# Two transformer layers and a delta-rule block on one core: modulation chunks moved to the feed-forward part, heads turned amid the v2 product, rotary halves swapped by transfers

## The chip, the cores and the metric

One core of a Trainium2 chip runs the whole program in one launch. Its engines are TensorE (PE in the profile), VectorE (DVE), ScalarE (ACT), GpSimd (POOL) and SyncE (SP, which issues most DMA transfers). The metric is the device time in microseconds, the median of several executions.

## What is computed

Two layers act on 256 tokens of width 1024, all in float32. Each has a mixer (a pooling branch and twelve attention heads of 64 in three dilation patterns), a feed-forward part of width 4096 and a gated embedding. A second block with a gated delta rule follows. It needs "modulation" columns, a product of two condition vectors with a weight of 1024 x 6144 that depends on nothing in the layers.

```python
def apply_partial_rotary(x, cos, sin):      # half = 8 of 64 columns
    x1 = x[..., :half]
    x2 = x[..., half:ROT_DIM]
    rot = jnp.concatenate([x1 * cos - x2 * sin, x2 * cos + x1 * sin], axis=-1)
    return jnp.concatenate([rot, x[..., ROT_DIM:]], axis=-1)
...
    for i in range(DEPTH):
        z = rmsnorm(h, norm1[i]) @ w_in[i]          # pool input, q, k, v
        q, k = rotary(q), rotary(k)
        attn_out = dilated_mixer(q, k, v)           # softmax within and across patterns
        h = h + jnp.concatenate([pool_out, attn_out], axis=-1) @ w_out[i]
        h = h + jnp.square(jax.nn.relu(rmsnorm(h, norm2[i]) @ w_up[i])) @ w_down[i]
        h = h + sigmoid(rmsnorm(h, norm3[i]) @ w_gate[i]) * (p[i] @ w_ple[i])
```

## The kernel before

**Weights as a stream.** Every weight is cut into chunks of 1 MB (`Stream`), loaded in one fixed order by SyncE's loop into four raw buffers (`RAW`). A load waits until the chunk four places earlier has been used up (`slot_free`). Most chunks are split: ScalarE writes a high part (`split_hi`, L521), DVE the low part (`split_lo`, L530), in two pieces of a half chunk each, into rings of four pieces (`PIECES`). PE then does three products per tile (high by high, low by high, high by low: L539 to L541), so a chunk is 48 matmuls of 256 columns, or 24 of 512. "Direct" chunks, those of the modulation weight and of the context, are multiplied from the raw buffer in full float32.

**Layer order.** Chunks 0 to 5 give q and k for three head pairs (`qk0` to `qk5`), 6 and 7 the first two thirds of v, 8 the pooling input u, 9 the last third of v (v2), 10 to 13 the output product, then up and down chunks of the feed-forward part alternate (14 to 45, `KIND`), then 46 to 51.

**Rotary.** ScalarE copies a product out of its bank (`z_raw`, L1737). PE multiplies it with a 128x128 matrix of 0, 1 and -1 (`rotate`, L1377), which swaps the two halves of eight rows and sets the sign. DVE multiplies the result with the sine table (`rotated`, L2156), GpSimd `z_raw` with the cosine table (L2546), DVE adds both (L2160). `z_raw`, `z_cos` and `z_sin` have two buffers each. PE does the rotation of product s behind product s + 1.

**Attention.** PE computes scores (L1386, L1387) into a ring of four banks (0 to 3, `low` and `CL`). DVE adds the mask and takes the maxima (`maxima`, L2168 to L2175), ScalarE the exponentials (`exps`, L1769), DVE scales them by weights for six heads at a time (`weights`, L2211). A table, `ATT_EXTRA`, and `attention_order` set what follows: "T" turns a head's probabilities on PE (L1295) and ScalarE copies them (L1792), "V" multiplies a head pair with v (L1438, L1440), ScalarE and DVE write the two parts of the result (L1800, L2265). Modulation work stands in the same order: "mod" is one chunk (L1317, two chunks are one pair), "modr" ScalarE's copy of a pair's rows (L1634), "modc" turns them into columns on PE (L1302), and DVE adds the bias (L2092). A second ring, banks 4 to 7 (`high` and `C`), serves the products, modulation and u. Layer 1's table has four context chunks in place of the modulation. `FFN_EXTRA` says what modulation work follows which chunk in layer 0's feed-forward part.

## Time and profile before

| what | us |
|---|---|
| median of three executions | 1394.09 (1393.87 to 1400.3) |
| profiled execution | 1391.02 |
| its span | 1389.0 |
| PE busy in it | 1302.8 |
| mean granted TensorE clock | 0.969 |

The span is the time from the first to the last instruction. Rows of the trace name an engine, a line of the kernel, the output and inputs by the program's names, and partitions x elements. A start is in microseconds from the span's start. Matmuls are pipelined and their ends are modelled, so steps are measured from start to start. "Idle before" in brackets is what the engine waited for.

### The profile page before, as it was taken

How to read it: one execution, taken by the hardware profiler on the slowest of the kernel's cores; microseconds unless marked ns; L12 is line 12 of the kernel's file. 1: busy time of each engine (PE TensorE's matmuls, PEld its weight loads, DVE VectorE, ACT ScalarE, POOL GpSimd, SP SyncE). 2: the span in 40 equal slices, each digit the busy share in tenths (PEclk: the TensorE clock that was granted, in tenths of full speed). 3: DMA queues.
4: the chain of work that ended last, by engine and by line, in shares of the span. 5: the costliest groups of instructions: out<-in, count | busy, mean ns of one | idle time of the engine just before them, and what ended most of it. 6: DMA issues, size and time to landing. Idle time of an engine off the chain costs nothing.

```text
span 1389.0 us, 22276 instructions
## 1 busy us (share of the span) xinstructions
PE 1302.8 (94%) x9222; PEld 1189.4 (86%) x9222; DVE 819.8 (59%) x1189; ACT 641.0 (46%) x950; POOL 124.6 (9%) x108
## 2 busy tenths in 40 slices
PE   7987999999999999789999989988889999999997
PEld 6964988888898889679999988988789998899996
DVE  6672464544685756676655586576644566654444
ACT  6353353443556635434444356454136453544443
POOL 0130000000002112140001030023310000000000
PEclk9997999999999999999999999999999999999999
DMA  9558467776554344234443444542004555355540
GB/s 320 164 189 267 141 221 242 242 245 227 178 181 152 92 138 136 91 122 152 152 152 123 159 145 122 152 122 92 30 1 135 183 173 179 130 189 190 190 151 31
DMA packets 163802, 218.74 MB, mean 157 GB/s; under 512 B 5016, under 2 KB 134902, under 8 KB 163574
## 3 DMA queue, kind: packets, MB, share of 16 engines
q1 hardware_dynamic: 161842, 215.15, 47.5%
q10 hardware_dynamic: 1860, 2.16, 0.5%
q8 instruction: 73, 1.20, 0.4%
q14 instruction: 27, 0.22, 0.1%
HBM read 216.26 MB, written 1.05 MB: 156 GB/s over the span
## 4 chain that ended last, share of the span: by engine, by line
PE 64%; issue 20%; DVE 6%; ACT 2%; POOL 2%; DMA 2%; DVEq 2%; POOLq 2%; ACTq 0%; SPq 0%
PE bank L539 17%; PE bank L540 17%; PE bank L541 17%; PE bank L602 2%; DVE w_lo L530 1%; PE bank L1317 1%; DMA w_raw<-in_w_mod 1%; PE bank L1295 1%; PE bank L1524 1%; PE bank L824 1%; PE bank L1377 1%; PE bank L812 1%; PE bank L1302 1%; DVEq L2171 1%; DMA arena<-in_vec_rows 1%
## 5 line engine op out<-in xcount | busy, mean ns | idle before, releaser
L530 DVE TENSOR_TENSOR w_lo<-w_raw,w_hi 128x1024 fp32r<-128x1024 f32 (+1 forms) x350 | 423.4, 1250 | 167.8 <-ACT w_hi L521 161.5
L539 PE MATMUL bank<-act_hi,w_hi 128*128 128x256 f32 x1744 | 505.0, 290 | 18.2 <-DVE act_lo L2139 5.1
L540 PE MATMUL bank<-act_lo,w_hi 128*128 128x256 f32 x1744 | 498.5, 286 | 0.0
L541 PE MATMUL bank<-act_hi,w_lo 128*128 128x256 f32 x1744 | 498.1, 286 | 0.0
L521 ACT ACTIVATE w_hi<-w_raw 128x1024 fp32r<-128x1024 f32 (+1 forms) x350 | 348.9, 1041 | 102.8 <-PE bank L541 89.9
L539 PEld LDWEIGHTS bank<-act_hi,w_hi 128*128 128x128 f32 x1744 | 339.7, 195 | 33.7 <-issue 19.4
L540 PEld LDWEIGHTS bank<-act_lo,w_hi 128*128 128x128 f32 x1744 | 339.9, 195 | 1.0 <-issue 0.5
L541 PEld LDWEIGHTS bank<-act_hi,w_lo 128*128 128x128 f32 x1744 | 339.5, 195 | 0.0
L539 PE MATMUL bank<-w_hi,side_hi 128*128 128x512 f32 (+1 forms) x392 | 151.1, 386 | 0.0
L540 PE MATMUL bank<-w_lo,side_hi 128*128 128x512 f32 (+1 forms) x392 | 148.6, 379 | 0.0
L541 PE MATMUL bank<-w_hi,side_lo 128*128 128x512 f32 (+1 forms) x392 | 148.4, 379 | 0.0
L1839 ACT ACTIVATE arena<-bank 128x512 f32<-128x512 f32 x32 | 19.1, 596 | 164.6 <-PE bank L541 164.6
L539 PEld LDWEIGHTS bank<-w_hi,side_hi 128*128 128x128 f32 x392 | 74.7, 191 | 14.6 <-issue 2.1
L541 PEld LDWEIGHTS bank<-w_hi,side_lo 128*128 128x128 f32 x392 | 74.4, 190 | 13.7
L540 PEld LDWEIGHTS bank<-w_lo,side_hi 128*128 128x128 f32 x392 | 74.7, 191 | 12.7 <-issue 0.5
L2296 DVE TENSOR_TENSOR arena<-arena 128x512 f32<-128x512 f32 x32 | 22.2, 695 | 105.3 <-ACTq L1840 105.3
L539 PE MATMUL bank<-side_hi,w_hi 128*128 128x256 f32 x208 | 63.7, 306 | 4.8 <-issue 2.7
L540 PE MATMUL bank<-side_lo,w_hi 128*128 128x256 f32 x208 | 60.2, 289 | 0.0
L541 PE MATMUL bank<-side_hi,w_lo 128*128 128x256 f32 x208 | 60.1, 289 | 0.0
L2546 POOL TENSOR_TENSOR arena<-arena 128x512 f32<-128x512 f32 x12 | 15.5, 1295 | 388.7 <-DVEq L2227 349.5
L539 PEld LDWEIGHTS bank<-side_hi,w_hi 128*128 128x128 f32 x208 | 41.3, 198 | 7.6 <-issue 5.2
L540 PEld LDWEIGHTS bank<-side_lo,w_hi 128*128 128x128 f32 x208 | 41.3, 199 | 1.7 <-issue 1.7
(323 smaller groups left out, 1540.8 us busy)
## 6 DMA issues: line engine op xcount, KB each, us to landing
w_raw<-in_w_in SPq DMA_DIRECT2D x40, 1024.0 KB, 5.8
w_raw<-in_w_up SPq DMA_DIRECT2D x32, 1024.0 KB, 6.4
w_raw<-in_w_down SPq DMA_DIRECT2D x32, 1024.0 KB, 5.0
w_raw<-in_w_mod SPq DMA_DIRECT2D x24, 1024.0 KB, 5.3
w_raw<-in_w_ffn_in SPq DMA_DIRECT2D x22, 1024.0 KB, 5.2
w_raw<-in_w_gate SPq DMA_DIRECT2D x20, 1024.0 KB, 5.3
w_raw<-in_w_ffn_out SPq DMA_DIRECT2D x11, 1024.0 KB, 5.3
w_raw<-in_w_out SPq DMA_DIRECT2D x8, 1024.0 KB, 8.0
```

The source lines that it names most:

```text
L521: nc.scalar.activation(whi[:, slot, 0:n], raw[:, st.slot(name), n * half:n * (half + 1)], ACT.Copy).then_inc(hi_ready, 1)
L530: nc.vector.tensor_tensor(wlo[:, slot, 0:n], raw[:, st.slot(name), n * half:n * (half + 1)], whi[:, slot, 0:n].bitcast(F32), ALU.subtract) ...
L539: nc.tensor.matmul(o, ahi, bhi, start=start, stop=False, skip_group_check=True)
L540: nc.tensor.matmul(o, ahi, blo, start=False, stop=False, skip_group_check=True)
L541: return nc.tensor.matmul(o, alo, bhi, start=False, stop=stop, skip_group_check=True)
L602: mm = nc.tensor.matmul(ps[bank][:, T * m:T * (m + 1)], raw[:, st.slot(name), at:at + P], act[:, k, :], start=k == 0, stop=k == KT - 1)
L812: mm = nc.tensor.matmul(ps[b][:, P * hh:P * (hh + 1)], h4(g_A[:, n, :])[:, hh, :], d_.x_new_of(n, hh, lv), start=True, stop=True)
L824: mm = nc.tensor.matmul(ps[b][:, P * hh:P * (hh + 1)], h4(z_sm[:, n, :])[:, hh, :], d_.t_new_of(n, hh, lv), start=True, stop=True)
L1295: tr = lambda o, x: nc.tensor.transpose(o, x, ident)
L1839: free(nc.scalar.activation(relu[j % 2], pair(b), ACT.Relu), b)
L2296: v.tensor_tensor(relu2[j % 2], relu[j % 2], relu[j % 2], ALU.mult).then_inc(S("relu2"), 1)
L2546: g.tensor_tensor(z_cos[s % 2], z_raw[s % 2], wide(tab_c, 2), ALU.mult).then_inc(S("z_cos"), 1)
```

## The change

The pairs 2 to 5 of the modulation (eight chunks, four row copies, four column turns) leave layer 0's attention and stand in its feed-forward part, where twelve chunks were before; there two chunks now go with every three weight chunks, from chunk 15 on, in place of two with every four from chunk 16. Pairs 0 and 1 stay. The v2 product is cut in two halves with the first two head turns in between, and these two write banks of the high ring. The last four heads' maxima come ahead of the copy of u on DVE, and their exponentials on ScalarE behind the first two head copies. The split of output chunks 10 and 11 in layer 0 is later. The first output product waits for its inputs one by one. The rotation on PE is gone: SyncE issues four transfers of 8 partitions x 512 elements per product from `z_raw` to `z_sin`, the sign is in the sine table, and `z_sin` is cleared once at the start.

```diff
+ROPE_MOVES = 16 * 4
...
-        ("ident", P), ("ones", P), ("rot", P), ("eps", 1), ("ln_q", 1), ("eps2", 1), ("even", 1), ("inv_freq", 1), ("pad", 1), ("mod_sum", 2),
+        ("ident", P), ("ones", P), ("eps", 1), ("ln_q", 1), ("eps2", 1), ("even", 1), ("inv_freq", 1), ("pad", 1), ("mod_sum", 2),
...
-            inv[m, 0] = np.float32(THETA) ** np.float32(-2.0 * (d % half) / ROT)
...
+            inv[m, 0] = (-1.0 if d < half else 1.0) * np.float32(THETA) ** np.float32(-2.0 * (d % half) / ROT)
...
-    out = [("v2", 0)] + extra.get("v2", [])
+    out = [("v2", 0)]
     for i, (b, g) in enumerate(pairs):
         out += [("T", HPG * g + 2 * b), ("T", HPG * g + 2 * b + 1)]
-        if i:
+        if i == 0:
+            out.append(("v2", 1))
+        else:
             out.append(("V", 2 * pairs[i - 1][1] + pairs[i - 1][0]))
-        if i == 4:
+        if i == 5:
...
-    {"v2": mod(0, 1, 2, 3), 0: [("modr", 0)] + mod(4, 5), 1: [("modr", 1), ("modc", 0)] + mod(6, 7),
-     2: [("modr", 2), ("modc", 1)] + mod(8, 9), 3: [("modr", 3), ("modc", 2)] + mod(10, 11),
-     4: [("modr", 4), ("modc", 3)], 5: [("modr", 5), ("modc", 4)], "V": [("modc", 5)]},
...
+    {1: mod(0, 1), 2: [("modr", 0)] + mod(2, 3), 3: [("modc", 0)], 4: [("modr", 1)], 5: [("modc", 1)]},
+    {1: [("ctx", 0)], 2: [("ctx", 1)], 3: [("conv", 0), ("ctx", 2)], 4: [("conv", 1), ("ctx", 3)], 5: [("conv", 2)],
+     "V": [("conv", 3), ("ba", 0)]})
...
-for j in range(6, MOD_PAIRS):
-    for at, entry in ((0, ("mod", 2 * j)), (2, ("mod", 2 * j + 1)), (3, ("modr", j)), (4, ("modc", j))):
-        FFN_EXTRA[0].setdefault(16 + 4 * (j - 6) + at, []).append(entry)
+for j in range(2, MOD_PAIRS):
+    for at, entry in ((0, ("mod", 2 * j)), (1, ("mod", 2 * j + 1)), (1, ("modr", j)), (2, ("modc", j))):
+        FFN_EXTRA[0].setdefault(15 + 3 * (j - 2) + at, []).append(entry)
...
-            early = 8 if layer == 0 else 3
+            early = 4 if layer == 0 else 3
...
-        def project_tokens(pe, name, bank):
-
-            for half in range(2):
+        def project_tokens(pe, name, bank, halves=(0, 1)):
+            for half in halves:
...
-                def rotate(s):
-                    wait("z_raw", s + 1, 6)
-                    b = CL(f"rot{s}")
-                    full(nc.tensor.matmul(ps[b][:, :], col("rot", 0, P),
-                                          z_raw[s % 2].rearrange("p m t -> p (m t)"), start=True, stop=True), b)
...
-                    else:
-                        if s == 1:
-                            ssq("ssq1", 1, CL("ssq1"))
-                        rotate(s - 1)
+                    elif s == 1:
+                        ssq("ssq1", 1, CL("ssq1"))
...
-                rotate(5)
...
-                        b = CL(f"pT{x}")
+                        b = C(f"pT{x}") if i < 2 else CL(f"pT{x}")
...
-                        b = C("v2")
-                        project_tokens(pe, (layer, 9), b)
+                        if x == 0:
+                            C("v2")
+                        project_tokens(pe, (layer, 9), banks.bank((layer, "v2")), (x,))
...
+                def cat_ready(f):
+                    first = max(f, 1)
+                    wait("cat_act", 1 + max(CAT_ORDER.index(x) for x in [0] + list(range(2, first + 1))), 7)
...
-                        if j == 0:
-                            wait("cat_act", 7, 7)
-                        project(pe, (layer, s), lambda m: (b, T * m), KT, all_hi, all_lo)
+                        project(pe, (layer, s), lambda m: (b, T * m), KT, all_hi, all_lo,
+                                cat_ready if j == 0 else None)
...
-                        W(f"rot{s - 2}")
+                        act.wait_ge(S(f"z_turned{s % 2}"), ROPE_MOVES * (layer * 3 + s // 2))
...
-                exps(8, 12)
...
-                        if layer != CTX_LAYER and i == 5:
-                            split_hi(act, chunk(layer, 10))
-                        if i == (3 if layer == CTX_LAYER else 9):
+                        if layer != CTX_LAYER and i == 9:
+                            split_hi(act, chunk(layer, 10), (0,))
+                        if layer == CTX_LAYER and i == 5:
                             split_hi(act, chunk(layer, 11))
...
-                    elif kind == "v2":
+                    elif kind == "v2" and x == 1:
+                        exps(8, 12)
...
+                if layer != CTX_LAYER:
+                    split_hi(act, chunk(layer, 10), (1,))
+                    split_hi(act, chunk(layer, 11))
...
-                    b = W(f"rot{s}")
-                    free(v.tensor_tensor(z_sin[s % 2], pair(b), wide(tab_s, 2), ALU.mult), b)
+                    dve.wait_ge(S(f"z_turned{s % 2}"), ROPE_MOVES * (layer * 3 + s // 2 + 1))
+                    v.tensor_tensor(z_sin[s % 2], z_sin[s % 2], wide(tab_s, 2), ALU.mult)
...
                 weights(0)
-
+                maxima(8, 12)
                 done(8)
                 b = bank("u")
                 free(v.tensor_tensor(win[0][:, :, PADW:], pair(b), wide(rstd_w[:, 0:T], 2), ALU.mult), b)
                 dve.drain().then_inc(S("u_ready"), 1)
-                maxima(8, 12)
+                weights(1)
                 if layer == CTX_LAYER:
                     split_lo(dve, chunk(layer, 10))
-                weights(1)
                 n = 0
                 for kind, x in ATT[layer]:
                     if kind == "modc":
...
-                    if n == 3:
-                        split_lo(dve, chunk(layer, 11 if layer == CTX_LAYER else 10))
-                    if n == 6 and layer != CTX_LAYER:
+                    if n == 3 and layer == CTX_LAYER:
                         split_lo(dve, chunk(layer, 11))
+                    if n == 5 and layer != CTX_LAYER:
+                        split_lo(dve, chunk(layer, 10), (0,))
...
+                if layer != CTX_LAYER:
+                    split_lo(dve, chunk(layer, 10), (1,))
+                    split_lo(dve, chunk(layer, 11))
...
+            for x in z_sin:
+                g.memset(x, 0.0)
...
+            def turn_halves(layer, s):
+                sp.wait_ge(S("z_raw"), layer * 6 + s + 1)
+                if layer or s >= 2:
+                    sp.wait_ge(S("qk_ready"), layer * 6 + s - 1)
+                half = ROT // 2
+                for i in range(2):
+                    for to, of in ((0, half), (half, 0)):
+                        to, of = HEAD * i + to, HEAD * i + of
+                        sp.dma_start(z_sin[s % 2][to:to + half], z_raw[s % 2][of:of + half]).then_inc(
+                            S(f"z_turned{s % 2}"), 16)
+            turns = {st.at[layer, 0] + s + 6: (layer, s) for layer in range(DEPTH) for s in range(6)}
             for n, (name, _, _) in enumerate(st.chunks):
+                if n in turns:
+                    turn_halves(*turns[n])
```

On PE in layer 0's attention, around the first V product (L1438, L1440; banks of the ring are shown). Before:

```order
L1317 MATMUL bank4<-w_raw,silu_c_cols 32x512 x8
L1317 MATMUL bank5<-w_raw,silu_c_cols 32x512 x8
L1295 MATMUL bank0<-consts_sb,arena 128x128 x3
L1295 MATMUL bank1<-consts_sb,arena 128x128 x3
L1317 MATMUL bank6<-w_raw,silu_c_cols 32x512 x8
L1295 MATMUL bank2<-consts_sb,arena 128x128 x3
L1295 MATMUL bank3<-consts_sb,arena 128x128 x3
L1438 MATMUL bank0<-arena 64x256
L1440 MATMUL bank0<-arena 64x128
```

Of the changed kernel, from the first V product's end to the fourth head pair (L1291 is the turn, L1313 the modulation, L1425 and L1427 the V product):

```order
L1427 MATMUL bank0<-arena 64x128
L1313 MATMUL bank6<-w_raw,silu_c_cols 32x512 x8
L1291 MATMUL bank1<-consts_sb,arena 128x128 x3
L1291 MATMUL bank2<-consts_sb,arena 128x128 x3
L1425 MATMUL bank3<-arena 64x256
...
L1313 MATMUL bank7<-w_raw,silu_c_cols 32x512 x8
L1291 MATMUL bank0<-consts_sb,arena 128x128 x3
```

Six modulation chunks stood ahead of the third head before, none does now; the fourth pair's first turn takes the bank that the first V product filled.

On SyncE's queue, the loads of layer 0's q, k and v stage. Before:

```order
L2594 DMA w_raw<-in_w_in 128x8x256 x3
L2602 DMA consts_sb<-in_consts 128x4608
L2594 DMA w_raw<-in_w_in 128x8x256 x5
L2594 DMA w_raw<-in_w_mod 128x4x512 x8
L2594 DMA w_raw<-in_w_out 128x8x256
```

Of the changed kernel (L2592 is the load, L2606 the swap):

```order
L2615 DMA consts_sb<-in_consts 128x4608
L2592 DMA w_raw<-in_w_in 128x8x256
L2606 DMA arena<-arena 8x512 x4
...
L2592 DMA w_raw<-in_w_mod 128x4x512
L2606 DMA arena<-arena 8x512 x4
L2592 DMA w_raw<-in_w_mod 128x4x512 x3
L2592 DMA w_raw<-in_w_out 128x8x256 x4
```

Four swaps stand ahead of each load from the seventh chunk on, six times in all; the first is behind the tables and one load.

On the same queue, the loads of layer 0's feed-forward part. Before:

```order
L2594 DMA w_raw<-in_w_mod 128x4x512
L2594 DMA w_raw<-in_w_down 128x2x1024
L2594 DMA w_raw<-in_w_up 128x8x256
L2594 DMA w_raw<-in_w_mod 128x4x512
L2594 DMA w_raw<-in_w_down 128x2x1024
L2594 DMA w_raw<-in_w_up 128x8x256
```

Of the changed kernel:

```order
L2592 DMA w_raw<-in_w_mod 128x4x512
L2592 DMA w_raw<-in_w_up 128x8x256
L2592 DMA w_raw<-in_w_mod 128x4x512
L2592 DMA w_raw<-in_w_down 128x2x1024
L2592 DMA w_raw<-in_w_up 128x8x256
```

One load in three was a modulation chunk, two in five are now, and they come over ten rounds of three weight chunks.

## Rows read from the trace of the kernel before

**Rows 1.** The page: busy time and share of PE; the clock in 40 slices, tenths.

```profile
PE 1302.8 (94%) x9222; PEld 1189.4 (86%) x9222; DVE 819.8 (59%) x1189; ACT 641.0 (46%) x950; POOL 124.6 (9%) x108
...
PEclk9997999999999999999999999999999999999999
```

**Rows 2.** Stages: stretch, its us, busy us of each engine, clock, DMA share, GB/s.

```profile
83.80:137.70 53.90, 40.39 (x281) 24.01 (x281) 24.89 (x84) 21.24 (x53) 10.47 (x12) 0.79 0.75 254
137.70:164.70 27.00, 25.51 (x192) 25.32 (x192) 10.61 (x13) 7.80 (x10) 0.00 (x0) 0.90 0.48 150
176.40:300.00 123.60, 121.93 (x790) 102.11 (x788) 63.51 (x64) 55.13 (x67) 0.00 (x0) 1.00 0.70 238
474.70:523.60 48.90, 48.70 (x297) 42.35 (x296) 30.42 (x90) 21.90 (x54) 11.96 (x12) 0.97 0.38 119
```

**Rows 3.** Waits in 83.8 to 137.7: total us, times, longest.

```profile
PE bank L1317 <- DMA w_raw<-in_w_mod: 11.6, 4, 7.1
```

**Rows 4.** Timeline of PE, layer 0's attention: start, us, line, operation.

```profile
114.28 0.88 PE L1295 MATMUL bank<-consts_sb,arena 128*128 128x128 f32 x6
115.09 0.66 PE L1438 MATMUL bank<-arena 128*64 128x256 f32 x4
...
115.90 1.05 PE L1302 MATMUL bank<-consts_sb,arena 128*128 128x2 f32 x8
116.88 1.06 PE L1317 MATMUL bank<-w_raw,silu_c_cols 128*32 128x512 f32 x8
125.00 1.93 PE L1317 MATMUL bank<-w_raw,silu_c_cols 128*32 128x512 f32 x8 [7.05 <-DMA w_raw<-in_w_mod]
...
129.54 1.13 PE L1450 MATMUL bank<-arena,pool_blocks 128*128 128x256 f32 x4
...
137.71 0.55 PE L539 MATMUL bank<-act_hi,w_hi 128*128 128x256 f32 x1 [1.91 <-issue]
```

**Rows 5.** Timeline of DVE: scaling of six heads, last maximum, scaling again.

```profile
84.81 2.85 DVE L2211 TENSOR_SCALAR arena<-arena 128x128 f32<-128x128 f32 x12
...
92.95 0.36 DVE L2175 TENSOR_SCALAR arena<-arena 128x2 f32<-128x2 f32 x1
...
97.59 4.12 DVE L2211 TENSOR_SCALAR arena<-arena 128x128 f32<-128x128 f32 x12
```

**Rows 6.** Timeline of PE around one rotation in layer 0.

```profile
36.54 0.28 PE L541 MATMUL bank<-act_hi,w_lo 128*128 128x256 f32 x1
36.66 1.02 PE L1377 MATMUL bank<-arena,consts_sb 128*128 128x512 f32 x2
...
37.63 0.28 PE L540 MATMUL bank<-side_lo,w_hi 128*128 128x256 f32 x1
```

**Rows 7.** Timeline of PE, last scores of layer 0.

```profile
81.78 0.46 PE L1386 MATMUL bank<-arena 64*128 64x128 f32 x2 [1.16 <-DVE arena L2169]
```

**Rows 8.** Timeline of DVE, low split of the fourth chunk.

```profile
35.38 2.35 DVE L530 TENSOR_TENSOR w_lo<-w_raw,w_hi 128x1024 fp32r<-128x1024 f32 x2
```

**Rows 9.** DMA issues to 240 us with landing; all raw loads of 14 to 60.

```profile
consts_sb<-in_consts SPq DMA_DIRECT2D x1, 2304.0 KB, 13.4
...
consts_sb<-in_consts SPq DMA_DIRECT2D x1, 196.0 KB, 2.5
...
DMA to landing us min/median/max: 5.1/6.4/14.4
```

**Rows 10.** Timeline of PE, feed-forward part of layer 0.

```profile
285.74 0.95 PE L1302 MATMUL bank<-consts_sb,arena 128*128 128x2 f32 x8
286.62 1.06 PE L1317 MATMUL bank<-w_raw,silu_c_cols 128*32 128x512 f32 x8
287.62 0.39 PE L539 MATMUL bank<-act_hi,w_hi 128*128 128x256 f32 x1
```

**Rows 11.** Timeline of PE, layer 1 behind the sixth product.

```profile
447.01 1.10 PE L1377 MATMUL bank<-arena,consts_sb 128*128 128x512 f32 x2 [1.99 <-ACT arena L1748]
```

**Rows 12.** Waits in layer 1's attention, 474.7 to 523.6.

```profile
ACT w_hi L521 <- DMA w_raw<-in_w_out: 4.1, 1, 4.1
```

More of the change, by code:

```diff
@@ L93, in const_tables @@
     put("ones", 1.0)
-    rot = np.zeros((P, P))
     half = ROT // 2
@@ L98, in const_tables @@
         d = m % HEAD
-        if d < half:
-            rot[m + half, m] = -1.0
-        elif d < ROT:
-            rot[m - half, m] = 1.0
         if d < ROT:
-            inv[m, 0] = np.float32(THETA) ** np.float32(-2.0 * (d % half) / ROT)
-    put("rot", rot)
+            inv[m, 0] = (-1.0 if d < half else 1.0) * np.float32(THETA) ** np.float32(-2.0 * (d % half) / ROT)
     put("inv_freq", inv)
@@ L282 @@
 V_ORDER = [x for k, x in ATT[0] if k == "V"]
+CAT_ORDER = [2 + x if k == "V" else 0 for k, x in ATT[0] if k in ("V", "pool")]
 def up_at(j):
```

2 lines of the change are left out of this document (removed).

## The prediction

> **What bounds the kernel now.** I read the page first: TensorE (PE) is busy 94% of a span of 1389.0 us, at full clock in all slices but one of the first four [rows 1]. So two things can move the time: work taken off PE, or gaps of PE that are closed. The table of stages says where the gaps are [rows 2]. Layer 0's attention (v2 product to the first output product, 83.8 to 137.7) lasts 53.9 us, of which PE is busy 40.4 at a mean clock of 0.79; the same stage of layer 1 lasts 48.9 us, PE busy 48.7. The feed-forward part of layer 0 is gapless (121.9 of 123.6 us), with the DMA engines at 0.70. So layer 0's attention is the hole. Its waits name the cause: PE waited 11.6 us for modulation chunks to land, 7.1 us of it at 125.0 [rows 3, 4]. The other 2 us of stillness are before 137.71 [rows 4]. The rest of the loss is the clock: row 125.00 shows two passes of a chunk at 1.93 us, row 116.88 the same work at 1.06 (1.2 against 2.4 GHz) [rows 4]. Twelve megabytes of modulation weights pass through four raw buffers there, beside a softmax that needs few loads.
>
> **1. Eight of twelve modulation chunks and four of six column turns leave layer 0's attention.** What is left there is bound by something else, so I walk the new order on the old time axis. Layer 0's stage starts when maxima free the banks of the last scores, at 83.76, as now. VectorE (DVE) scales the first six heads at 84.81 to 87.66, then takes the last four maxima at once (the u copy, 0.7 us, is moved behind them), which costs the same as now and keeps them near 93; the scaling of the last six heads starts at 97.59 now and ends 4.12 later, at 101.7 [rows 5]. PE meanwhile does both halves of v2, three head pairs, two V products and four modulation chunks. Its fourth pair needs heads that are scaled, and the bank of the first V product (four claims back on a ring of four banks), which DVE frees only behind all of that scaling: so it starts near 101.7, maybe 1 us earlier. From there PE has three head pairs at 0.81 (114.28 to 115.09), four V products at 0.81 (115.09 to 115.90), two column turns at 0.98 (115.90 to 116.88) and the pool product at 1.13 [rows 4]: 2.4 + 3.2 + 2.0 + 1.1 = 8.7 us. The last hand-off (ScalarE's high part, DVE's low part, with half of the first output chunk's split, about 1.2 us, queued ahead of it on DVE) adds 2. Together 101.7 + 8.7 + 2.0 = 112.4, or a stage of 28.6 us in place of 53.9: **-25.3**. Ends: if the scaling isn't what binds, PE's own work remains, v2 5.8 (48 slots of 0.12, the step from 36.54 to 36.66 [rows 6]) plus six pairs, six V, four chunks at 1.0, two turns and the pool, 22.6 us: -31. If the clock falls in the gaps, the tail of 8.7 takes about 1.8 times as long (1.93 against 1.06) and the waits with it: 36 us, -18.
>
> The output products after it ran 27.0 us with a granted clock of 0.90 [rows 2], since PE came from a standstill. With less of that I take **-1.0** (0 to -2.5).
>
> **2. They arrive in the feed-forward part.** PE is gapless there, so each is paid in full: a chunk 1.0 us (286.62 to 287.62), a column turn 0.88 (285.74 to 286.62) [rows 10]. 8 x 1.0 + 4 x 0.88 = **+11.5**. Is there room to load them? Five loads of 1.05 MB now go with three PE steps: 3 x 5.67 (a pair of up and down takes 11.3) + 2 x 1.0 + 0.9 = 19.9 us, so 263 GB/s. The stage moves 238 GB/s at a share of 0.70 [rows 2], 340 at a full share; so the share rises to 0.77. With four raw buffers a load is issued as soon as the fourth chunk before it is split or used, which I work out as 9 us or more before its own split, against 5.1 to 6.4 us that most loads take to land [rows 9]. I take no stall; if each of the ten periods loses 1 us, +10. ScalarE's copy of the rows now waits for the second chunk at once, ahead of the split of the next-but-one weight chunk: about 1.6 us of a slack of 3.
>
> **3. The rotary swap leaves PE.** A rotation costs PE 36.66 to 37.63, less one slot of 0.12 for the product's matmul between: 0.85 us [rows 6]; there are six per layer. ScalarE's z_raw copy stays; after it four transfers of 8 partitions x 2 KB swap rows, then DVE multiplies as before. In layer 0 five of the six lie ahead of the first v chunk's end: 5 x 0.85 = 4.25 us. The sixth gives nothing: from that end a chain over ScalarE and DVE (values, split, maxima) sets when the last scores find a bank, PE waits 1.16 us for it at 81.78 already [rows 7], and it would only wait longer. Against that stands the start. SyncE's queue issues the first swap near 25.5 behind the tables, which take 13.4 us to land, and behind a weight chunk (14.4 at most) issued at 20.6 [rows 9]; so I expect it at 33 to 35.5. DVE stands at it, and behind it in DVE's queue is the low split of the fourth weight chunk, which starts at 35.38 even now [rows 8] and takes 1.2 for its first half. PE, 0.85 us earlier, wants it at 35.8. So its first half is ready at 36.6 at best and 38.2 at worst (35.5 and two vector steps of 0.7 to 0.9 behind the swap, then 1.2): a new gap of 0.8 to 2.4 us, I take 1.6. Net **-2.65** (-3.5 to -1.8).
>
> No row shows a transfer from SBUF to SBUF. The smallest load with a landing, 196 KB, took 2.5 us, the slowest of 1 MB 14.4 [rows 9]. I take 3 to 5 us, nearer to the small one, since in the steady state the load ahead of it on the queue was issued 3 us before. DVE can wait until 7.5 us after the issue before the split behind it is late, so this is hidden. The Trainium skill, DMA: Bandwidth & Descriptors, "Anatomy of one DMA", gives about 2 us of fixed cost for a DMA on GpSimd's path, mostly the write receipt; by it the sum would be the same. The same page, "Queues, rings and completion order", says that each engine takes a ring's descriptors in order, which speaks against the change: the swap can't overtake the tables. No row here shows small transfers behind large ones; by that rule alone the gap would be the 2.4 us end, and the total 0.8 us longer.
>
> In layer 1 four rotations lie ahead of the sixth product: 3.4, of which 0.5 goes because the fourth chunk's split is just in time there too. The fifth waited 1.99 us for ScalarE at 447.01 [rows 11], and that and its 0.85 vanish from PE; but the attention's start is again set by the chain over values, splits and maxima, of which only about 0.4 shrinks. So the stage starts 3.3 us earlier, **-3.3** (-6 to -1), not 7.1. What is late next is the bank of the last scores, as in layer 0.
>
> **4. Layer 1's attention in its new order.** The same PE work is done (48.7 of 48.9 busy). The context chunks start later, so output chunk 11 lands later; ScalarE waits 4.1 us for it even now [rows 12], hidden under a context product of 7 us. I count **0** (-1 to +2), and if that cover is short by a load, up to +2.
>
> **The sum.** -25.3 - 1.0 + 11.5 - 2.65 - 3.3 + 0 = -20.75. The profiled execution took 1391.0, which gives 1370.3. It lies 3.1 us under the median of the three runs, 1394.1, and I keep that distance: **1373.3 us**.
>
> **Rivals.**
> - *The loads collide in the feed-forward part.* For it: 263 GB/s wanted against 238. Against: share 0.77. It costs 1 us in each of ten periods: 1383.
> - *Attention is a softmax chain with a cold clock.* For it: 0.79 in this stage [rows 2], and the new order has PE waits near 92 and 100. The stage takes 36 us, 7.5 more, and the output stage gains nothing: 1382.
> - *The tail is shorter still.* If scaling runs without GpSimd beside it (2.85 against 4.12 for the same twelve instructions [rows 5]) and hand-offs hide: 5 us less, 1368.
> - *Slower: swaps land late.* DVE's queue holds the split of the chunk three ahead behind each swap. If a swap lands L us after its issue, that split is late once L passes 7.5; the delay feeds the next z_raw three products later. At L = 14.4, the slowest load here, each round of three products loses 6.9 us. Twelve swaps are four rounds: +27.6, and the sum gives 1401. For it: one queue with the 1 MB loads. Against: those take 5.1 to 6.4 us, and only the first meets the tables.
> - *The chunks' removal does nothing because they fill waits that remain.* Then 1373.3 + 25.3 - 8 = 1391. Against: 11.6 us of waits on exactly these loads [rows 3].
>
> **Chances.** Forecast with its own bounds 0.75, collision 0.07, cold chain 0.07, shorter tail 0.04 (1363 to 1369), fills 0.03, slower swaps 0.04. The range must leave out no more than 2 in 10 and takes in both ends of the attention stage: 1364 to 1384. Half a per cent, about what a measurement tells from no change, is 7 us: faster than 1387 in 0.93, within in 0.03, slower in 0.04.
>
> **What would show it.** The stage of layer 0's attention at 28 to 29 us with no wait on w_mod, and the fourth head pair waiting for DVE. In the feed-forward part, periods of three steps near 19.9 us and the granted clock at 1.00. No 128x512 rotation on PE; a PE wait for w_lo of 1 to 2 us near 36; DVE's rotary product waiting for the first swap only. PE's wait in the last scores longer than 1.16 in both layers. I am wrong if PE waits for w_mod in the feed-forward part, if SyncE's swaps land later than 7.5 us, or if layer 0's attention stays above 36 us.

## The result, and the profile after

| kernel | median us (range) | before, same chip | ratio (95%) |
|---|---|---|---|
| changed, first measurement | 1379.85 (1378.0 to 1383.3) | 1395.9 | 0.9893 (0.987 to 0.9916) |
| changed, again (e1) | 1381.9 (1379.6 to 1387.0) | 1397.4 | 0.9908 (0.9882 to 0.9934) |

The change makes the kernel 1.0% faster: 13 to 15 us by the ratios, 15 to 16 by the medians. The forecast was 1373.3, in a range of 1364 to 1384. So the direction and the range held, but the time lies 6.5 us above the forecast, and of the 20.75 us of the sum 5 to 8 did not come. The executions of the kernel before spread from 1387.7 to 1400.6 over the chips used (one of 3209.6 us, in the slow state, is left out), and their mean granted clock goes with it (0.969 to 0.974 up to 1392.7, 0.962 to 0.967 from 1397.2 on). The profiled one, 1391.0, lies at the low end, and the profiled one of the changed kernel, 1383.3, at the high end of its own. So the two traces differ by 7.7 us where the medians differ by 16. Sizes of single stages below come from traces; what a whole kernel is worth comes from the ratios.

The stages of the changed kernel, columns as in [rows 2]. They are, in turn: first product to the first v product of layer 0, on to its v2 product, layer 0's attention, its output products, a piece of its feed-forward part, layer 1's attention, and the first output product of layer 1.

```profile
15.99:57.86 41.87, 39.21 (x299) 38.92 (x300) 29.89 (x31) 22.83 (x30) 7.65 (x5) 0.96 0.77 253
57.86:84.15 26.29, 24.86 (x195) 22.25 (x193) 19.15 (x59) 15.51 (x42) 1.85 (x1) 1.00 0.51 163
84.15:116.90 32.75, 24.88 (x186) 18.48 (x185) 22.51 (x75) 17.07 (x48) 10.88 (x12) 0.90 0.40 129
116.90:141.65 24.75, 23.25 (x192) 23.08 (x193) 14.41 (x17) 9.58 (x12) 0.00 (x0) 1.00 0.65 207
155.00:280.00 125.00, 124.43 (x812) 102.57 (x811) 61.82 (x66) 53.67 (x66) 0.00 (x0) 1.00 0.79 266
460.53:513.07 52.54, 49.12 (x297) 42.27 (x297) 33.56 (x92) 22.28 (x56) 12.51 (x12) 0.98 0.39 121
513.07:521.05 7.98, 7.98 (x50) 7.98 (x51) 3.28 (x12) 4.79 (x6) 2.48 (x3) 0.72 0.00 1
```

Layer 0's attention went from 53.9 us to 32.75, at a granted clock of 0.90 in place of 0.79. Layer 1's, which was gapless at 48.9, went to 52.54. All waits of PE of 0.6 us or more in layer 0's attention of the changed kernel (total us, times, longest):

```profile
PE bank L1291 <- DVE act_lo L2258: 5.0, 1, 5.0
...
PE bank L535 <- DVEq L2266: 1.5, 1, 1.5
...
PE bank L1313 <- DVE arena L2234: 0.7, 1, 0.7
...
PE bank L1438 <- DVE act_lo L2258: 0.6, 1, 0.6
```

The 11.6 us for w_mod [rows 3] are gone. In their place stands one wait of 5.0 us: the transpose of the fourth head pair needs the bank of the first V product, which DVE frees only behind its scaling of the last six heads. That scaling, on DVE's timeline, with the same work of the first six heads ahead of it; the third row is one of three small steps between:

```profile
85.20 2.84 DVE L2205 TENSOR_SCALAR arena<-arena 128x128 f32<-128x128 f32 x12
...
93.72 0.69 DVE L2234 TENSOR_TENSOR arena<-bank,rstd 128x512 f32<-128x512 f32 x1
...
95.82 1.03 DVE L2192 TENSOR_TENSOR arena<-arena 128x4 f32<-128x4 f32 x1
...
98.26 6.15 DVE L2205 TENSOR_SCALAR arena<-arena 128x128 f32<-128x128 f32 x12
104.33 0.97 DVE L2258 TENSOR_TENSOR act_lo<-bank,act_hi 128x256 fp32r<-128x256 f32 x2
```

Twelve equal instructions take 2.84 us once and 6.15 the other time; before, the second set took 4.12 [rows 5]. The u copy (93.72) releases GpSimd's window sums, which ran from 94.61 to 106.5 and so beside all of it. Before, they ran from 88.45 to 100.0: the first five us beside the maxima, only the last 2.4 beside the scaling. GpSimd's timeline before, then after:

```profile
88.45 4.83 POOL L2552 TENSOR_TENSOR arena<-arena 128x512 f32<-128x512 f32 x4 [29.76 <-DVEq L2241]
...
96.62 3.36 POOL L2562 TENSOR_TENSOR arena<-arena 64x256 f32<-64x256 f32 x4
```

```profile
94.61 4.82 POOL L2550 TENSOR_TENSOR arena<-arena 128x512 f32<-128x512 f32 x4 [33.99 <-DVEq L2235]
...
103.28 3.27 POOL L2560 TENSOR_TENSOR arena<-arena 64x256 f32<-64x256 f32 x4
```

PE behind its wait, and the first three us there in the columns of [rows 2]: the granted clock was 0.50.

```profile
104.89 1.51 PE L1291 MATMUL bank<-consts_sb,arena 128*128 128x128 f32 x6 [5.03 <-DVE act_lo L2258]
106.33 1.13 PE L1425 MATMUL bank<-arena 128*64 128x256 f32 x4
```

```profile
104.89:107.82 2.93, 2.93 (x14) 1.90 (x15) 0.42 (x1) 0.98 (x2) 1.55 (x3) 0.50 1.09 348
```

Layer 0's start did not get shorter: 68.12 us from the first product to v2 before, 68.16 after. DVE stood at the first swap, and PE behind it (DVE's timeline, then PE's, then SyncE's queue with the four transfers of the first swap and of the second):

```profile
36.28 0.69 DVE L2150 TENSOR_TENSOR arena<-arena 128x512 f32<-128x512 f32 x1 [3.75 <-DMA arena<-arena]
...
37.67 3.45 DVE L526 TENSOR_TENSOR w_lo<-w_raw,w_hi 128x1024 fp32r<-128x1024 f32 x2
```

```profile
39.03 0.35 PE L535 MATMUL bank<-side_hi,w_hi 128*128 128x256 f32 x1 [2.54 <-DVE w_lo L526]
```

```profile
25.50 4.99 SPq L2606 DMA_DIRECT2D arena<-arena  x4
31.52 0.38 SPq L2592 DMA_DIRECT2D w_raw<-in_w_in  x1
31.95 2.65 SPq L2606 DMA_DIRECT2D arena<-arena  x4
```

And layer 1's attention got two waits of PE and one long wait of ScalarE for w_out, which was 4.1 [rows 12]:

```profile
ACT w_hi L517 <- DMA w_raw<-in_w_out: 13.9, 1, 13.9
...
PE bank L598 <- issue: 2.2, 1, 2.2
...
PE bank L1291 <- DVE act_lo L2258: 1.2, 1, 1.2
```

### The profile page after: what moved, and what is told of

Same layout as the page of the kernel before. It is cut to its first block, busy times and chain, and to the rows that moved or that the text cites. A ratio compares the mean times of both kernels' runs of the same rounds, so it can differ in the third digit from the quotient of the medians.

```text
span 1381.5 us, 22278 instructions
## 1 busy us (share of the span) xinstructions
PE 1296.9 (94%) x9198; PEld 1188.4 (86%) x9198; DVE 826.3 (60%) x1189; ACT 640.7 (46%) x950; POOL 127.8 (9%) x110
## 4 chain that ended last, share of the span: by engine, by line
PE 60%; issue 21%; DVE 8%; ACT 3%; DVEq 2%; POOL 2%; POOLq 2%; DMA 2%; ACTq 1%; SPq 0%
PE bank L535 17%; PE bank L537 16%; PE bank L536 16%; DVE w_lo L526 2%; PE bank L598 2%; PE bank L1313 1%; PE bank L820 1%; PE bank L1291 1%; PE bank L1515 1%; DVEq L2165 1%; PE bank L808 1%; ACT w_hi L517 1%; DMA arena<-in_vec_rows 1%; DVE arena L2205 1%; PE bank L1298 1%
## 5 line engine op out<-in xcount | busy, mean ns | idle before, releaser
L535 PEld LDWEIGHTS bank<-act_hi,w_hi 128*128 128x128 f32 x1744 | 339.6, 195 | 31.0 <-issue 19.9
L2544 POOL TENSOR_TENSOR arena<-arena 128x512 f32<-128x512 f32 x12 | 18.6, 1560 | 367.5 <-DVEq L2221 331.6
```

Of the source, the lines that this page charges most:

```text
L535: nc.tensor.matmul(o, ahi, bhi, start=start, stop=False, skip_group_check=True)
L2544: g.tensor_tensor(z_cos[s % 2], z_raw[s % 2], wide(tab_c, 2), ALU.mult).then_inc(S("z_cos"), 1)
```

## The experiments

My theory after the result: the moved chunks are the gain; the swaps gave little because PE only arrives earlier at what ScalarE and DVE set; and the shortfall is two things that the new order did, DVE's queue in layer 0 and everything in layer 1. The rivals stand in the expectations. All runs are compared by their ratio to the kernel before on the same chip. The interval of each ratio is about 0.0025 to either side, 3.5 us, so a difference between two kernels is known to some 5 us only. Where it is smaller, the reading rests on the stages of the traces.

**e1, the changed kernel again.** No edit.

> The changed kernel once more, unchanged, beside the kernel before. The two profiles differ by 7.5 us, the medians by 16. Theory 'the profiled executions lie at opposite ends of the scatter': the median comes out at 1378 to 1382 again, 14 to 17 us under before, and the stages of a second profile repeat within 0.5 us except for waits on DMA (layer 1's attention 52.5, its first output product 8.0). Rival 'the profile is right and the first four times were lucky': the medians differ by 8 to 10 us.

1381.9 us, 15.4 under before by the medians, 12.9 by the ratio: the first theory. Layer 1's attention repeats (52.7). Layer 0's took 34.2, which is 1.4 longer, and first product to v2 67.35, 0.8 shorter, so stages repeat to about 1.5 us and not to the 0.5 that I expected.

**e3, chunks only.** In the kernel before, the new tables of modulation steps and nothing else:

```diff
-    {"v2": mod(0, 1, 2, 3), 0: [("modr", 0)] + mod(4, 5), ...
+    {1: mod(0, 1), 2: [("modr", 0)] + mod(2, 3), 3: [("modc", 0)], 4: [("modr", 1)], 5: [("modc", 1)]},
...
-for j in range(6, MOD_PAIRS):
+for j in range(2, MOD_PAIRS):
```

> The kernel before with only the modulation chunks and column turns of layer 0 moved to its feed-forward part (positions as in the changed kernel); the v2 product stays whole and first, all maxima and exponentials ahead of it as before, rotation on TensorE. Theory 'the chunks are the gain': layer 0's attention falls from 53.9 to 31 to 34 us, the output products win 2.3, the feed-forward part pays 12.6: the whole is 10 to 13 us faster than before, 1382 to 1385. Rival 'the cut of v2 and the heads amid it matter as much': attention stays at 38 to 40 us and the whole is 5 us faster than before, near 1390.

1388.1 us, ratio 0.9940: 8.4 us under before by the ratio, 9.3 by the medians, so more than half of the gain is the chunks alone, a little short of the 10 to 13 expected. Attention took 35.85 us in the trace, between the theory's 31 to 34 and the rival's 38 to 40. With the old order of heads DVE's second scaling took 4.12 us again, since the u copy ran ahead of the last maxima and GpSimd had started at 87.4.

**e2, the rotation back on TensorE.** The changed kernel without the swaps:

```diff
+                def rotate(s):
+                    wait("z_raw", s + 1, 6)
+                    b = CL(f"rot{s}")
+                    full(nc.tensor.matmul(ps[b][:, :], col("rot", 0, P), ...
...
-                if n in turns:
-                    turn_halves(*turns[n])
```

> The changed kernel with the rotary swap back as a product on TensorE (the transfers on SyncE's queue and DVE's wait for them are gone); the moved chunks and the order of attention stay. Theory 'in layer 0 the swaps gave nothing': PE pays 0.85 us for each rotation again but no longer waits 2.5 us for w_lo near 39 nor runs half a product at half clock (1.5 us), so the v2 product of layer 0 starts at 83.5 to 84.5 as in the changed kernel (84.15), layer 1 gives back 3.75 us, and the whole is 3 to 4 us slower than the changed kernel: near 1384. Rival 'as the prediction has it': the swaps are worth 2.65 + 3.3, so 6 us slower, 1386. Rival 'the small transfers also disturb the loads and the queue': same as the changed kernel or faster, 1378 to 1380.

1382.3 us, ratio 0.9907 against 0.9908: the medians show no loss, where 3 to 4 us were expected, and the interval leaves room for that. In the traces layer 0 takes 67.9 us from first product to v2 with the rotation and 67.35 without. Layer 1 shows where the gain goes. From layer 0's first output product to layer 1's first scores takes 328.85 us with the rotation, 321.16 without: 7.7 won. From there to v2 it is 20.43 against 22.70: 2.3 given back, 0.5 of it in a wait of PE for a split and most of the rest in the u product, whose first half ran at a clock near half (4.5 us in place of 3.0). This profiled execution lay 3 us over its own median, so I take the direction from it and not the size.

**e11, the swaps alone**, in the kernel before:

> The kernel before with only the rotary swap done by transfers; modulation chunks and the order of attention as before. Theory 'the swaps are worth little': taking them out of the changed kernel cost 0.4 us by the medians and 3.7 by the traces, all of it in layer 1; so 0.5 to 4 us faster than before, the first scores of layer 0 not earlier than 62.5 (64.0 before), layer 1's scores earlier by 6 to 7 us but its v2 product only by 4 to 5. Rival 'as the prediction has it': 6 us faster, 2.65 of it in layer 0. Rival 'the swaps cost elsewhere': same or slower.

1390.9 us, ratio 0.9969 (0.995 to 0.9988): 4.3 us, the upper end. Layer 0 from first product to v2: 68.3 us (68.1 before). From layer 0's first output product to layer 1's v2: 333.4 in place of 337.0. So what the traces show of a gain is in layer 1, and it is not the whole account: layer 0's attention, whose order is that of before, took 56.5 us in this trace in place of 53.9, and the two profiled executions are 0.3 us apart.

**e4 and e5, what holds the first swap up.** e4 loads the tables (2.3 MB) four chunks later on SyncE's queue; e5 has ScalarE issue them on its own, near the same time as SyncE did:

```diff
-                if n == 4:
+                if n == 8:
                     sp.dma_start(kt[:, first_tables:NK], ...
```
```diff
+                if layer == 0:
+                    act.dma_start(kt[:, first_tables:NK], ...
                 square_tiles()
```

> The changed kernel with the load of the tables on SyncE's queue four chunks later (behind chunk 8 in place of chunk 4), so that the first swap does not stand behind it. Theory 'the tables hold the first swap up': DVE's wait for the first swap (3.75 us at 36.3) falls under 1, PE's wait for w_lo of 2.5 us at 39 and the half product at half clock go, and the first v product starts near 54.5 in place of 57.9; the attention starts 1 to 3 us earlier. Rival 'the weight chunk ahead of it holds it up, or the first swap's own start': the wait stays over 2.5 us. Rival 'the chain over ScalarE and DVE ahead of the last scores takes it back': the first v product starts 3 us earlier but v2 only 0 to 0.5.

> The changed kernel with the load of the tables issued by ScalarE, on its own queue, near 20 us in place of by SyncE. With the load four chunks later the wait did not go, it moved: DVE waited 6.8 us for the fourth swap at 55.1 and PE 3.7 us behind it. Theory 'a swap that stands behind a large load on the same queue lands only when that load has': on another queue no swap waits for the tables; DVE's wait for the first swap (3.75 us) falls under 1.5, PE's wait for w_lo at 39 (2.5) under 0.5, the first scores come near 60.5 in place of 62.2 to 63.7. Rival 'it is the shared DMA engines, whichever the queue': the first swap lands as late as before, PE waits 2 us or more again. For the whole both give at most 1 to 3 us, since the last scores of the stage wait for DVE.

e4: 1385.3, ratio 0.9925, 2.4 us slower than e1 by the ratios, within the intervals. The wait moved with the load. SyncE's queue and DVE's timeline of e4:

```profile
42.84 0.58 SPq L2615 DMA_DIRECT2D consts_sb<-in_consts  x1
43.51 2.65 SPq L2606 DMA_DIRECT2D arena<-arena  x4
```

```profile
31.84 1.84 DVE L2150 TENSOR_TENSOR arena<-arena 128x512 f32<-128x512 f32 x1
...
55.10 0.69 DVE L2150 TENSOR_TENSOR arena<-arena 128x512 f32<-128x512 f32 x1 [6.80 <-DMA arena<-arena]
```

The first swap met no tables and no wait. The fourth, issued right behind them at 43.5, was there only at 55.1, and PE waited 3.7 us for w_lo. So the tables hold up the swap that follows. But e5 (1380.3, ratio 0.9902) refutes that it is the shared queue alone: with the tables on ScalarE's queue DVE still waited 3.52 us for the first swap and PE 2.57. The Trainium skill, DMA: Bandwidth & Descriptors, "Queues, rings and completion order", says that a DMA engine takes turns between the rings that have work, one packet each. That fits a swap slowed by a load on another ring. The weight chunks of its own queue were ahead of the first swap in every run, in e4 too, where DVE did not wait. So it was the tables that held it up, from either queue: in the 5 us behind the swap's issue (25 to 30) the DMA engines were busy all the time in e5, 0.96 of it in the changed kernel and 0.44 in e4. Turn-taking itself is not shown.

**e6, the bank freed earlier.** In DVE's queue, the low parts of the first two V products stand ahead of the first and the third scaled head:

```diff
-                    for hd in heads(batch):
+                    for j, hd in enumerate(heads(batch)):
+                        if between and j in (0, 2):
+                            between(j // 2)
...
-                weights(1)
+                weights(1, low_part)
```

> The changed kernel with DVE's low parts of the first two V products put amid its scaling of the last six heads: one ahead of the first head, one ahead of the third, in both layers; nothing is left out. Theory 'PE's 5.03 us before 104.89 are the bank of the first V product, which DVE frees behind all of its scaling': PE's fourth pair starts at 99.5 to 101 and the attention of layer 0 falls from 33 to 34 us to 29.5 to 31. Rival 'the scaled heads themselves are what PE waits for': the scaling runs beside GpSimd at 0.5 us an instruction, PE waits for each pair, and the stage falls by 1 us or less.

1375.2, ratio 0.9868 (0.984 to 0.9895). Layer 0's attention:

```profile
84.92:111.80 26.88, 23.68 (x185) 17.59 (x185) 22.03 (x75) 16.82 (x47) 10.76 (x12) 0.94 0.48 157
```

and PE's two waits near the fourth and sixth pair, with the scaling:

```profile
101.52 0.55 PE L1291 MATMUL bank<-consts_sb,arena 128*128 128x128 f32 x3 [0.38 <-DVE arena L2207]
106.31 0.84 PE L1291 MATMUL bank<-consts_sb,arena 128*128 128x128 f32 x6 [0.93 <-DVE act_lo L2270]
```

```profile
99.58 1.89 DVE L2207 TENSOR_SCALAR arena<-arena 128x128 f32<-128x128 f32 x4
101.94 3.89 DVE L2207 TENSOR_SCALAR arena<-arena 128x128 f32<-128x128 f32 x8
```

The scaling is as slow as before this edit (5.8 us of instructions), yet the stage fell from 33 or 34 us to 26.9: six to seven us, more than expected. The fourth pair started at 100.59, as the theory had it. PE needs the heads two at a time and they come fast enough; what it stood for was the bank, behind all of them. In layer 1, where the edit stood too, it won nothing (53.6 us).

**e7, GpSimd kept off the scaling.** The signal to GpSimd moved behind it:

```diff
-                dve.drain().then_inc(S("u_ready"), 1)
+                dve.drain()
                 weights(1)
+                dve.drain().then_inc(S("u_ready"), 1)
```

> The changed kernel with DVE's signal to GpSimd (windows may start) moved behind DVE's scaling of the last six heads; the copy itself stays in place. Theory 'GpSimd's work beside it stretches DVE's': the scaling takes 2.84 us as for the first six heads, not 6.15, and its three small steps 0.3 + 0.16 + 0.31 in place of 1.19 + 1.03 + 0.76, so it ends near 99 in place of 104.4, and PE's fourth pair starts near 99.5. But GpSimd's windows take 11.9 us from there, so the pool product is ready near 111 at best and PE waits for it: the stage falls by 2 to 3 us only, from 33 to 34 to 31. Rival 'DVE is slow for another reason': the scaling stays at 6 us with GpSimd idle, and the stage grows by 4 us.

1381.1, ratio 0.9911: no gain in the time. The theory holds for DVE and for the new wait, though not for the stage, which fell less than the 2 to 3 us expected. DVE's small step and scaling with GpSimd idle, GpSimd's first window sums, and PE at the pool product:

```profile
96.16 0.16 DVE L2192 TENSOR_TENSOR arena<-arena 128x4 f32<-128x4 f32 x1
...
97.27 2.84 DVE L2205 TENSOR_SCALAR arena<-arena 128x128 f32<-128x128 f32 x12
```

```profile
100.30 4.82 POOL L2551 TENSOR_TENSOR arena<-arena 128x512 f32<-128x512 f32 x4 [40.50 <-DVEq L2237]
```

```profile
112.66 0.80 PE L1438 MATMUL bank<-arena,pool_blocks 128*128 128x256 f32 x1 [6.07 <-POOLq L2562]
```

The scaling is back at 2.84 and the small step at 0.16 (1.03 beside GpSimd). PE's wait for the bank is gone, but it now stands 6.07 us for the windows. The stage took 32.4. The Trainium skill, SBUF — State Buffer, "SBUF: two separate sides", describes a port pair that DVE and GpSimd lock in turn for a whole instruction, the other being blocked. For DVE the traces agree: the small step grew by 0.87 us, less than one window sum of 1.2 (4.82 for four). That GpSimd is blocked in turn they don't show: all its windows took 11.9 us beside the scaling (94.61 to 106.55) and 12.3 in e7 (100.30 to 112.55). Nor is all of DVE's work slowed. Its last four maxima, which read one operand from a PSUM bank or reduce, took 1.16 us a head beside the window sums before and 1.16 without them in the changed kernel.

**e8, layer 1's attention as before.** Order, u copy and the places of the splits, in layer 1 alone:

```diff
-    {1: [("ctx", 0)], 2: [("ctx", 1)], 3: [("conv", 0), ("ctx", 2)], 4: [("conv", 1), ("ctx", 3)], ...
+    {"v2": [("ctx", 0)], 0: [("ctx", 1)], 2: [("ctx", 2)], 3: [("conv", 0)], 4: [("ctx", 3), ("conv", 1)], ...
```

> The changed kernel with layer 1's attention in the order of the kernel before (whole v2 product first, context product behind it, pool behind the fifth pair, the u copy ahead of the last four maxima, the split of output chunk 11 two pairs earlier); layer 0 and all swaps stay. Theory 'the new order costs layer 1 what it has no waits to win': the stage falls from 52.6 to 49 us, PE's wait of 2.2 us at 471 for the bank of u goes, ScalarE's wait for w_out falls from 14 to about 4 us, and the first output product goes from 8.0 to 6.0: 4 to 5.5 us in all, 1377. Rival 'the loss in layer 1 comes from the swaps' earlier start, not from the order': the stage stays over 51.5 us.

1377.3, ratio 0.9877 (0.9848 to 0.9906), by the ratios 4.3 us better than e1 and 2.2 better than the first measurement, both within the intervals; the stage itself is clear. The stage, and the wait of ScalarE in it:

```profile
462.37:510.62 48.25, 48.05 (x297) 41.71 (x297) 31.36 (x92) 22.24 (x56) 11.84 (x12) 0.99 0.40 125
```

```profile
ACT w_hi L518 <- DMA w_raw<-in_w_out: 3.7, 1, 3.7
```

The stage lost 4.3 us, and the rival falls: the swaps were in this kernel too. The one part of my expectation that failed is the first output product of layer 1, which ran at 0.65 of the clock again (8.4 us).

**e9, e10 and e12, both edits together**: e6's in layer 0 only and e8's. e10 adds the tables in four parts behind chunks 7 to 10; e12 has the rotation back on TensorE.

> The changed kernel with two edits together: DVE's low parts of the first two V products amid its scaling in layer 0 only, and layer 1's attention in the order of the kernel before. The edits lie in different stages. Theory 'they add': one gave 1375.2 and the other 1377.3 where the changed kernel gave 1381.9, so 1381.9 - 6.7 - 4.7 = 1370.5; layer 0's attention 27 us, layer 1's 48.3. Rival 'what one edit wins is scatter or is given back later': 1374 or more.

> As the kernel with both edits, and the tables (2.3 MB) loaded in four parts of 0.58 MB by SyncE behind chunks 7 to 10, each behind the swap that is issued ahead of that chunk. On another queue the tables held the first swap up as much as on the same one (DVE 3.5 us, PE 2.6 us); four chunks later they held the fourth up by 6.8 us. Theory 'what counts is how many bytes are still to be moved when a swap is issued': the first swap meets none of them, and the later ones 0.58 MB at most, so DVE waits under 1 us at the first and under 2.5 at any other, PE's wait for w_lo near 39 goes, and the first scores come at 60 or earlier in place of 62; the whole is 1 to 2.5 us faster than with both edits alone. Rival 'each of the four parts holds up the swap behind it by its own 1.7 us and more': no wait of PE is saved in the sum, same time. Rival 'the masks land too late for the first maxima': DVE waits for tables near 68, slower.

> As the kernel with both edits, but the rotary swap as a product on TensorE again: all of the change and the two edits except the swaps. Theory 'the swaps are worth little': 0.5 to 4 us slower than with both edits, 1371 to 1374.5. Rival 'as the prediction has it': 6 us slower, 1376.5. Rival 'nothing or a loss': as fast as with both edits or faster.

| kernel | median us (range) | ratio (95%) |
|---|---|---|
| e9 both | 1372.5 (1372.1 to 1374.7) | 0.9842 (0.9817 to 0.9866) |
| e10 tables spread | 1374.4 (1371.6 to 1376.8) | 0.9851 (0.9827 to 0.9876) |
| e12 rotation on PE | 1374.3 (1370.0 to 1381.0) | 0.9858 (0.9828 to 0.9888) |

e9 beats both kernels: 9.2 us under e1 by the ratios (0.0066 of 1395), 7.1 under the first measurement of the changed kernel. The two edits add: 0.0040 and 0.0031 by their own ratios, 0.0066 together, though the median is 2 us above the 1370.5 expected. Its two stages are those of the single edits:

```profile
83.97:110.69 26.72, 23.52 (x185) 17.43 (x185) 21.93 (x74) 16.66 (x45) 10.77 (x12) 0.94 0.50 158
456.05:504.26 48.21, 48.01 (x297) 41.66 (x297) 31.31 (x92) 22.27 (x56) 11.87 (x12) 0.99 0.39 124
```

e10 won nothing, where 1 to 2.5 us were expected. DVE found the first swap without a wait, and PE's wait near 39 fell from 2.74 to 1.03 and the first scores came 46.2 us behind the first product in place of 47.9, but from there to v2 took 22.3 in place of 20.6. DVE now waited 3.96 us for the third swap, issued behind the first part of 0.58 MB. e12 is 2.2 us worse than e9 by the ratios, within the intervals.

## Why the prediction was right, and where it was not

| term | forecast | traces of the changed kernel (first, e1) |
|---|---|---|
| layer 0's attention | -25.3 | -21.2, -19.8 |
| its output products | -1.0 | -2.3 (first) |
| feed-forward part | +11.5 | +12.6 (first) |
| layer 0's q/k/v | -2.65 | 0.0, -0.8 |
| layer 1's q/k/v | -3.3 | -3.75 (first) |
| layer 1's attention | 0 | +3.6, +3.75 |
| layer 1's first output product | not in the sum | +2.0, +2.2 |

The first column adds up to -20.75, the traced terms of the first trace to -9, and its profiled execution lies 7.7 us under that of before. Medians and ratios give 13 to 16. So 4 us or more of the gain is in no term: it is the level of the profiled executions, and no run resolves it further.

**The hole and its price: right.** The 11.6 us for w_mod vanished, and what bound the stage next was the bank of the first V product, as the working said. Up to the fourth pair the forecast was 17.9 us (83.8 to 101.7), measured 20.7 (84.15 to 104.89). From there 10.7 against 12.0. That difference is the clock behind the wait: the fourth pair's turns and the V product after them took 2.93 us at a granted clock of 0.50, where the sum had 1.62.

**The step that failed in it** is "(the u copy, 0.7 us, is moved behind them), which costs the same as now". The copy's own 0.7 us does, but it starts GpSimd, and 12 us of window sums, whose first five had run beside the maxima at no cost to DVE, fell on the scaling and the small steps ahead of it. I read 4.12 in [rows 5] as the price of scaling beside GpSimd; it was the price of being beside it for a part. I even had 2.85 for the same instructions one row higher, and treated it as a rival that could only shorten the tail. The scaling took 6.15 us in place of 4.12: 2.0 of the 2.8 us. e7 shows the cause. No run puts the u copy back ahead of the maxima in the new order, so what that alone would win is open. e6 shows more: the scaled heads and the bank stood side by side in the sum, as if both bound, and only the bank did.

**Arrivals in the feed-forward part: right.** Ten column turns stand from 166.89 to 348.92, a period of 20.2 us in the mean (20.0 to 21.0) where 19.9 was forecast. That is most of the 1.1 us between +12.6 and +11.5. The clock was 1.00 and the DMA share 0.74 to 0.79. The one stall in it is 0.57 us at 174.99, so the collision rival falls.

**Layer 0's swaps: wrong by the whole term.** The kind of loss was right: PE waited 2.54 us for w_lo behind the first swap. The estimate was 1.6, its worst case 2.4. The swap was mis-sized: it was expected at 33 to 35.5 and came at 36.28, 10.8 us after its issue at 25.50. And one price was missing: PE's half product behind the wait ran near half clock (4.4 us in place of 2.95). So of the 4.25 us of five rotations 2.54 and 1.5 went again, which leaves 0.2. (In e1 the clock stayed up there, which is most of its -0.8.) The split behind the swap ran beside GpSimd's product, but only its second half was slowed (2.31 us; 1.22 for the first), and PE did not wait for that. Two of the signs failed as well. DVE waited not for the first swap only, but for the third (2.56) and the fifth (1.12) too; before, it had waited there 2.6 for PE's rotation. And PE's wait in the last scores did not grow (1.17 us, 1.16 before). Over all traces the way from the first product to v2 is 68.1 us in the mean with the rotation on PE (67.9 to 68.1, four traces: before, e2, e3, e12) and 68.1 with the swaps (67.0 to 69.6, nine traces, e4 aside). Within a scatter of some 2.5 us the five rotations of 0.85 that leave PE there buy nothing. Only a longer wait shows (e4, 71.4).

**Layer 1's swaps.** The traces gave the -3.3 that was forecast or more (-3.6 in e11, -5.4 between e2 and e1 and between e12 and e9). But the last scores were not what was late next, as the working had it: PE's wait in them fell from 1.42 us to 0.82. What was given back there is told at e2. The three pairs of ratios put the value of all twelve swaps at 0, 2.2 and 4.3 us, each to within some 3 to 5 us. So 5.95 was probably too high, by the traces through layer 0's 2.65; the rest can't be sized closer.

**Layer 1's attention: a term taken as 0 that was +3.6.** I had named the later w_out load, "+2 if that cover is short by a load", and not the other half. The u copy behind the last maxima also frees the bank that the first context product claims, and PE stood 2.2 us for it: the copy ran from 470.09 for 0.69 us and PE started at 470.88. (The profile names no releaser; e8, without the wait, bears it out.) That product came later, so did its raw buffer. The load of output chunk 11 was issued 26.1 us into the stage (486.62) in place of 21.7, and ScalarE's queue stood 13.9 us with the evacuation of a V product behind. e8 takes all of it back. Even with PE busy 48.7 of 48.9 us an order is not free to change: the gaplessness was the old order's.

**The level.** The sum was made against a profiled execution at the low end of its kernel and then shifted by 3.1 to the median. That was a little short: the later medians of the kernel before are 1394.4 to 1397.4, 3.4 to 6.4 above it. That the time came within 6.5 us of the forecast says little for the sum, then: its errors in the traced terms come to 11.7 us, and the level of the two executions hid some 5 of them.

**Left open:** the first output product of layer 1 ran at full clock (5.8 us) in the traces of before, e3, e5 and e6, and at 0.65 to 0.77 of it (7.3 to 8.4 us) in the ten others. The same order stands in both groups, so the +2.0 need not be the change's, and I can't say what it is. Also open is where the new order of heads pays: by the ratios of e3 and e2 it is worth 4.6 us over both layers, but their traces show -2.3 in layer 0's attention and +2.7 in layer 1's, and e3's profiled execution lies 6.6 us under its own median.

## What to carry to other kernels

Before an instruction is moved, list whom it signals and what the released engine does next: a copy of 0.7 us decided which of DVE's steps 12 us of GpSimd's work fell on. Where an engine waits for a bank, free the bank amid the long operation and not behind it; that one edit was worth 5.6 us by the ratios to e1, all twelve swaps 0 to 4.3. Work taken off the busiest engine ahead of a stage that two other engines pace returned here as a wait, and a product near half clock behind the wait took 1.5 us more.

## What the runs showed of the hardware

- Beside GpSimd's fp32 tensor operations, DVE's twelve 128x128 scalings take 6.15 us and without them 2.84; a 128x4 product takes 1.03 in place of 0.16. The low split of a weight chunk took 3.45 in place of 2.35. The maxima (a mask added from a PSUM bank, a reduction) are not slowed: 1.16 us a head either way.
- Four transfers of 16 KB from SBUF to SBUF cost SyncE's queue 2.65 us, 0.66 each; the first four, issued behind the tables, cost it 4.3 to 5.8, and 2.8 where the tables came later (e4, e10). With a weight chunk ahead of them DVE had the data 5.3 to 5.8 us after the issue began (third swap of e4 and of the changed kernel); behind 2.3 MB of tables 11.6 us after (43.51 to 55.10), and a different queue for the tables didn't help (3.52 us of wait; 3.75 on the same queue).
- Spreading the 2.3 MB over four parts moved DVE's waits for swaps in layer 0 from the first on to the third and later ones (3.96, 2.5, 1.7 and 2.3 us) and raised their sum to 10.4 us from 7.7 in e9.
